# A fused two-layer mixer on one core: gate columns Z projected in the attention pairs, the state stage reordered, and the X tiles' weight sums made by GpSimd

## The chip, the cores and the metric

One core of a Trainium2 chip runs the whole program as one launch. The metric is device time in microseconds (us), lower is better. TensorE (PE) does the matrix products, VectorE (DVE) and ScalarE (ACT) the elementwise work, GpSimd (POOL) and SyncE (SP) issue DMAs. Everything is float32.

## The reference, cut to what matters

Three blocks follow one another over 256 tokens of width 2048. The change lies in the first, which mixes neighbourhood attention with a state-space part:

```python
p = h @ w_in                                   # h: 256 x 2048; columns Q, gate A, Z, K, V, X|B|C, dt
pc = hc @ w_in[:, base:]                       # the same for the 256 context tokens (K, V, X, B, C, dt alone)
ya = neighbourhood_attention(q, k, v, kc, vc, rpb) * silu(gate_a)
xs, B, C = silu(dw_conv(X|B|C));  dt = softplus(dt_raw + dt_bias)
y_ssd = bidirectional_ssd(...)                 # 8 groups, each 256 columns of X and Z, 128 of B, 128 of C
yz = (y_ssd + d * xs) * silu(z)                # z = Z columns of p
yb = yz * rsqrt(mean(yz * yz, per group) + EPS) * ssm_norm_g
out = concatenate([ya, yb]) @ w_out
```

So Z is used only at the end of each group of the state part, and depends on nothing in it.

## The kernel before

The engines run programs of their own, written out by hand in order, and meet at semaphores. Weight tiles of 2048 x 256 (2 MB) go through four slots `w[0..3]` in SBUF. The SP queue loads a slot as soon as PE has counted enough finished products in `acc_full`; the counts of each stage stand in `PHASES` (how many products a round has, and after which of them each slot is free).

The attention stage is eight pairs of heads (`na(i)`). Each pair has four weight tiles (Q, gate, K, V) and six units (`na_unit`), because K and V are also projected for the context tokens. A unit is one 256 x 256 x 2048 product in seven instead of eight block products of 128 x 128 x 1024 (56 matmuls with 128 moving columns), for which VectorE makes three block sums of the weights (`sums_one`, `sums_two`, placed in `w[3]`, counted in `na_t`) and combines the seven results afterwards (`na_combine`). ScalarE copies the results out of PSUM (`na_staging`). Between the units PE does the scores, transposes and values of the pair before. GpSimd loads the second layer's modulation weights through `xT` in the background, VectorE adds them up (`late_part`).

The state stage is eight groups (`ssd(g)`). From group 1 on, PE's order in a group is: X in four parts (`ssd_x`, seven block products with 256 moving columns, sums made by VectorE's `x_weights`), and between them the work of the group before: pairs of B and C (`s_cb`), state products (`s_st`), `ssd_within` 0 to 3 and `ssd_across`. Then B and C of this group (`featured`), Z in two halves of 16 matmuls with 256 moving columns (`tokened`), the transposes of the group before's result (`ssd_features`), and the transposes of this group's X and B into `wide` and `bank[5]` (counted in `s_xt`). VectorE's order is `x_weights`, `to_the_end`, `mask_cb`, `all_heads` (`decays` and `weights` for four heads, counted in `s_wm`), the X results, five-tap convolutions (`conv`, `conv_silu`), `combine` (the group before's result, which ends with `s_yz` and the scaling by `rz`), and at the end of the group the copies out of the transposes.

After group 7 PE starts the output projection (`out_first`, `out_half`) beside the last group's state work. The slot loads of that stage are in `out_proj` on SP.

Of the kernel before, what the change touches and what calls it, by code (L numbers as in the profile page):

```python
# [115 lines left out]
def build(nc, ins, out, scratch):  # L116
    x_scratch = nc.dram_tensor("x_columns", (P, DC * T), F32, kind="Internal").ap()
    y_scratch = nc.dram_tensor("na_columns", (P, DC * T), F32, kind="Internal").ap()
    f_scratch = nc.dram_tensor("ssd_columns", (P, DC * T), F32, kind="Internal").ap()
    with ExitStack() as ctx:  # L120
        program(nc, ctx, ins, out, scratch, x_scratch, y_scratch, f_scratch)


def program(nc, ctx, ins, out, scratch, x_scratch, y_scratch, f_scratch):
# [48 lines left out]

    IDENT, ANTI, ONES, BIG_GE = const("ident"), const("anti"), const("ones"), const("big_ge")
    FOLD = const("fold")
# [34 lines left out]
    staged0, partial0 = L(7, P), L(2, P)  # L210
    yout = L(2, T)
    late_rows = L(32)
# [86 lines left out]
    PHASES = [("na", 8, 12, [2, 4, 8, 12]), ("ssd", 8, 8, [4, 6, 8, 8]), ("out", 4, 4, [2, 2, 4, 4]),  # L299
# [77 lines left out]
    def na_filled(n, whole=True):  # L377

        return 12 * (n // 4) + (2, 4, 8, 12)[n % 4] - (0 if whole else 1)
# [28 lines left out]
    def loads(s, phase, i):  # L408
        g = GROUPS[phase]
        extra = 0  # L410
        if s == 1:
            extra = 16 * (i + 1) if phase == "ssd" else (16 * 8 if g > GROUPS["ssd"] else 0)
        if s == 3 and g > GROUPS["ssd"]:
            extra = -16 * 8
        extra += 16 * ((3, 3, 2, -8)[s] + EARLY[s])
        return 16 * (g + 1) + 16 * i + extra
# [8 lines left out]
    early_taken, late_taken, late_sum, late_added, x_moved, y_saved, y_back, wdt_in = (sem(n) for n in ("early_taken", "late_taken", "late_sum", "late_added", "x_moved", "y_saved", "y_back", "wdt_in"))  # L425
# [9 lines left out]
    def names(prefix, *which):  # L435
# [3 lines left out]
    (na_ss, na_rs, na_lnfree, na_kq, na_hk_in, na_sc, na_max, na_p, na_pn, na_pt, na_pts, na_po, na_y,  # L439
     na_g) = names("na", "ss", "rs", "lnfree", "kq", "hk_in", "sc", "max", "p", "pn", "pt", "pts", "po", "y", "g")  # L440
    (d_full, d_x, d_abs, d_log, d_a, d_cs, d_csout, d_rows, d_rowsb, d_store, d_toend, csb_in) = names(
        "dt", "full", "x", "abs", "log", "a", "cs", "csout", "rows", "rowsb", "store", "toend", "csb_in")
# [10 lines left out]
    (na_ge, s_ce, s_cl, s_zl, s_ze, sc_e, g2_x, g2_l, sb_ge, ch_ge) = (  # L453
        sem(f"sig_{n}") for n in ("na", "ssd_c", "ssd_cl", "ssd_zl", "ssd_z", "sc", "g2_x", "g2_l", "sb", "ch"))
# [12 lines left out]
    def _(gp):  # L467
# [25 lines left out]
        iterations(gp, 8, late_chunks)  # L493


    @block.sync
    def _(sp):
# [39 lines left out]
        def slot_free(phase, i, s):  # L537

            if isinstance(i, int) and i == 0:
                prev = EARLIER[phase]  # L540
                if phase == "ssd":
                    return sp.wait_ge(acc_full, na_filled((30, 31, 29)[s]))
# [24 lines left out]
        for n in (0, 2, 1, *range(3, 32)):  # L567
# [4 lines left out]
            at = (COL_Q, COL_GATE, COL_K, COL_V)[n % 4] + (n // 4) * TILE  # L572
# [8 lines left out]
            if n % 4 == 1 and n > 4:  # L581
                na_biases(n // 4 - 1)
        na_biases(7)

        def ssd(i):
            at = [columns(i, COL_X), columns(i, COL_Z)]
            half = [COL_B + i * P, COL_C + i * P] if isinstance(i, int) else [
                sp.snap(i * P + COL_B), sp.snap(i * P + COL_C)]
            slot_free("ssd", i, 0)
            load(0, w_in[:, :, ds(at[0], TILE)])  # L590
# [3 lines left out]
            slot_free("ssd", i, 2)  # L594
            load(2, w_in[:, :, ds(at[1], TILE)])
# [3 lines left out]
        def out_proj(i):  # L599

            at = [sp.snap(i * (2 * TILE) + n * TILE) if not isinstance(i, int) else (2 * i + n) * TILE for n in range(2)]
            for s in range(SLOTS):
# [4 lines left out]
                load(s, w_out[s % 2][:, :, ds(at[s // 2], TILE)])  # L607
                if is_first(i) and s == 0:

                    sp.wait_ge(y_saved, 16 * 8)  # L610
                    sp.dma_start(yT[:, 0:DC, :].rearrange("p a b -> p (a b)"), y_scratch).then_inc(y_back, 16)
                    sp.wait_ge(f_saved, 16 * 6)
# [55 lines left out]
    def _(pe):  # L668
# [145 lines left out]
        def na_values(a, h):  # L814
            pe.wait_ge(na_pts, 2 * a + h + 1)
            pe.wait_ge(n_made, 6 * a + 6)
# [22 lines left out]
        def na_unit(i, u, midway=None):  # L839
# [43 lines left out]
        def na(i):  # L883
# [22 lines left out]
            na_unit(i, 5, lambda: na_sums(i, 2, ksq[:, 1, :]))  # L906

# [34 lines left out]

        def ssd_x(g, part):
# [5 lines left out]
            if part == 0:  # L949
                pe.wait_ge(s_made, 12)  # L950
                product(a, quarter(0, 0, 1), XC(0, 0))
                last = product(b, quarter(0, 1, 1), XC(0, 1))
            elif part == 1:
                pe.wait_ge(x_t, 3 * g - 1)
                product(a, t2, XC_SUM[2])
                last = product(b, quarter(0, 0, 0), XC_SUM[3])
# [4 lines left out]
            else:  # L961
                pe.wait_ge(x_t, 3 * g)
# [3 lines left out]
        def ssd(g):  # L966
            first = is_first(g)
            s = g - 1
            loaded(0, "ssd", g)
            if first:  # L970
                dst = accumulate("ssd", 0, g)

                featured(dst[:, :], 0, 0, T + TC, None, range(EIGHT))
                na_scores(7, 0)
                featured(dst[:, :], 0, 0, T + TC, None, range(EIGHT, DC)).then_inc(acc_full, 3)
# [3 lines left out]
                featured(dst[:, :], 0, 1, T + TC, None, range(EIGHT))  # L979
                na_values(7, 0)  # L980
                na_transposes(7, 1)
                featured(dst[:, :], 0, 1, T + TC, None, range(EIGHT, DC)).then_inc(acc_full, 1)
# [3 lines left out]
            else:  # L986
                ssd_x(g, 0)
                pe.wait_ge(s_xtk, g)
                pe.wait_ge(s_silu, 4 * g)
                for jb in range(2):  # L990
                    last = mm(bank[2][:, jb * T:(jb + 1) * T], bT[:, jb * P:(jb + 1) * P], cmT[:, :])
                last.then_inc(s_cb, 1)
                ssd_x(g, 1)
# [28 lines left out]
            pe.wait_ge(s_silu, 4 * g + 3)  # L1022
            if not first:
                pe.wait_ge(s_t1, 2 * s + 2)
            for tb in range(4):
                for c in range(2):
                    tr(wide[:, tb * TILE + c * P:tb * TILE + (c + 1) * P], xc[:, c, tb * P:(tb + 1) * P])
            for jb in range(2):
                last = tr(bank[5][:, jb * P:(jb + 1) * P], bT[:, T + jb * P:T + (jb + 1) * P])
            last.then_inc(s_xt, 1)  # L1030

        def out_half(cb, ch, half):
# [4 lines left out]
            for kc in range(DC):  # L1037
# [4 lines left out]
        def out_first(cb, ch):  # L1042
# [3 lines left out]
            out_half(cb, ch, 0)  # L1046

        def ssd_apply(s, beside):
            ssd_across(s)
            for r in range(4):  # L1050
                if r == 2:
                    beside()
                ssd_within(s, r)
# [27 lines left out]
        iterations(pe, 8, ssd)  # L1081
        pe.wait_ge(s_xtk, 8)
        pe.wait_ge(s_silu, 32)
        for jb in range(2):
            last = mm(bank[2][:, jb * T:(jb + 1) * T], bT[:, jb * P:(jb + 1) * P], cmT[:, :])
        last.then_inc(s_cb, 1)
        pe.wait_ge(y_back, 16)
        out_first(0, 0)
# [5 lines left out]
        last.then_inc(s_st, 1)  # L1094
        out_first(0, 1)
        ssd_apply(7, lambda: out_first(1, 0))
        out_first(1, 1)
# [362 lines left out]
    def _(act):  # L1460
# [154 lines left out]
        for i in range(8):  # L1615
            na(i)
# [1309 lines left out]
```

## Time and profile before

| | |
|---|---|
| median of 3 runs | 2649.34 us (2647.27 to 2649.52) |
| profiled execution, its own time | 2646.37 us |
| span of that execution | 2644.7 us |
| granted TensorE clock, mean | 0.998 |
| PE / DVE / ACT / POOL busy | 98% / 65% / 18% / 2% |
| HBM | 171 GB/s over the span |

The profile comes from one execution. Its start times are us from the start of the span. A line in the timeline view is a run of like instructions on one engine: start, duration from the first one's start to the last one's end, line of the kernel, what is written from what, and count. A float32 matmul of the program is two MATMUL instructions in these views, so a count of 64 is 32 matmuls. Idle time before a run stands in brackets with what ended it.

### The profile page before, as it was taken

How to read it: one execution, taken by the hardware profiler on the slowest of the kernel's cores; microseconds unless marked ns; L12 is line 12 of the kernel's file. 1: busy time of each engine (PE TensorE's matmuls, PEld its weight loads, DVE VectorE, ACT ScalarE, POOL GpSimd, SP SyncE). 2: the span in 40 equal slices, each digit the busy share in tenths (PEclk: the TensorE clock that was granted, in tenths of full speed). 3: DMA queues.
4: the chain of work that ended last, by engine and by line, in shares of the span. 5: the costliest groups of instructions: out<-in, count | busy, mean ns of one | idle time of the engine just before them, and what ended most of it. 6: DMA issues, size and time to landing. Idle time of an engine off the chain costs nothing. (4 is left out here: it accounts for less than half of the span.)

```text
span 2644.7 us, 41302 instructions
## 1 busy us (share of the span) xinstructions
PE 2592.1 (98%) x17269; PEld 2305.3 (87%) x17269; DVE 1713.3 (65%) x2832; ACT 476.6 (18%) x922; POOL 60.9 (2%) x85
## 2 busy tenths in 40 slices
PE   5899999999999999999999999999999999999999
PEld 2399999999996877777778998888889999999999
DVE  6878778878775666666655535555566655556643
ACT  2121111212121222222220002111111112122211
POOL 1000000000000000000000000000000000000000
PEclk9999999999999999999999999999999999999999
DMA  9956666557554333333354546655654555555542
GB/s 379 366 168 224 197 218 202 189 187 242 193 170 141 97 104 111 115 115 115 115 207 159 171 149 191 188 152 170 190 165 155 154 165 149 152 156 156 166 149 74
DMA packets 382238, 453.96 MB, mean 172 GB/s; under 512 B 20884, under 2 KB 352264, under 8 KB 381064
## 3 DMA queue, kind: packets, MB, share of 16 engines
q1 hardware_dynamic: 350176, 352.03, 43.5%
q0 software_dynamic: 21776, 83.89, 8.8%
q10 hardware_dynamic: 10136, 15.86, 1.7%
q8 instruction: 117, 1.92, 0.3%
q14 instruction: 33, 0.27, 0.0%
HBM read 443.56 MB, written 8.19 MB: 171 GB/s over the span
## 5 line engine op out<-in xcount | busy, mean ns | idle before, releaser
L670 PE MATMUL bank<-hT,w 128*128 128x128 f32 (+2 forms) x4192 | 653.7, 314 | 4.2 <-ACT hT L1462 2.7
L670 PEld LDWEIGHTS bank<-hT,w 128*128 128x128 f32 x4192 | 548.4, 192 | 101.4 <-issue 87.4
L670 PE MATMUL bank<-yT,w 128*128 128x128 f32 (+1 forms) x3776 | 526.4, 299 | 1.5 <-DVE yT L2459 1.0
L670 PEld LDWEIGHTS bank<-yT,w 128*128 128x128 f32 x3776 | 493.2, 192 | 23.5 <-DVE yT L2459 1.2
L670 PE MATMUL bank<-w,hT 128*128 128x256 f32 (+2 forms) x2816 | 485.9, 332 | 3.3 <-ACT hT L1462 2.2
L670 PEld LDWEIGHTS bank<-w,hT 128*128 128x128 f32 x2816 | 438.8, 191 | 49.0 <-issue 9.5
L1462 ACT ACTIVATE work<-bank 128x512 f32<-128x512 f32 (+3 forms) x294 | 150.8, 521 | 1191.1 <-PE bank L670 1093.1
L1462 ACT ACTIVATE work<-work 128x512 f32<-128x512 f32 (+4 forms) x287 | 166.0, 584 | 279.4 <-DVE work L2309 156.1
L2134 DVE SCALAR_TENSOR_TENSOR work<-xT,silc,work 128x512 f32<-128x512 f32 x240 | 180.3, 751 | 28.2 <-DMA xT<-in_ada_w 21.4
L670 PE MATMUL bank<-work,hT 128*128 128x256 f32 x768 | 168.5, 379 | 0.0
L670 PEld LDWEIGHTS bank<-work,hT 128*128 128x128 f32 x768 | 145.4, 190 | 19.5
L2570 DVE TENSOR_TENSOR work<-w 128x2048 f32<-128x2048 f32 x16 | 36.7, 2292 | 152.8 <-PE bank L670 139.6
L670 PE MATMUL bank<-hT,work 128*128 128x128 f32 x1136 | 134.9, 275 | 0.0
L670 PEld LDWEIGHTS bank<-hT,work 128*128 128x128 f32 x1136 | 130.8, 192 | 0.0
L2524 DVE TENSOR_TENSOR work<-yT 128x128 f32<-128x128 f32 x37 | 10.8, 293 | 178.5 <-ACT yT L1462 178.5
L670 PEld LDWEIGHTS bank<-w,yT 128*128 128x128 f32 x1024 | 116.9, 192 | 3.8 <-issue 3.8
L670 PE MATMUL bank<-w,yT 128*128 128x128 f32 x1024 | 118.2, 275 | 0.0
L670 PE MATMUL bank<-work 128*128 128x256 f32 (+2 forms) x368 | 103.2, 408 | 2.9 <-DVE work L2495 1.6
L2309 DVE SCALAR_TENSOR_TENSOR work<-work,colp 128x512 f32<-128x512 f32 (+1 forms) x128 | 87.7, 685 | 15.0
L1462 ACT ACTIVATE yT<-bank 128x512 f32<-128x512 f32 (+1 forms) x63 | 35.6, 566 | 253.4 <-PE bank L670 221.9
L670 PEld LDWEIGHTS bank<-work 128*128 128x128 f32 x368 | 64.0, 191 | 17.6 <-issue 9.1
L670 PE MATMUL wide<-w,work 128*2 128x512 f32 x128 | 58.4, 604 | 14.3 <-DMA w<-in_ada_w 14.3
(253 smaller groups left out, 2541.8 us busy)
## 6 DMA issues: line engine op xcount, KB each, us to landing
w<-in_na_ssd_w_in SPq DMA_DIRECT2D x47, 2048.0 KB, 11.3
xT<-in_ada_w POOLq DMA_DIRECT2D x64, 1024.0 KB, 8.8
w<-in_sc_w_in SPq DMA_DIRECT2D x32, 2048.0 KB, 13.5
w<-in_w_in SPq DMA_DIRECT2D x32, 2048.0 KB, 10.7
w<-in_na_ssd_w_out SPq DMA_DIRECT2D x16, 2048.0 KB, 9.5
w<-in_na_ssd_w_in SPq DMA_DIRECT2D x18, 1024.0 KB, 8.9
w<-in_sc_w_out SPq DMA_DIRECT2D x8, 2048.0 KB, 8.6
w<-in_w_out SPq DMA_DIRECT2D x8, 2048.0 KB, 8.8
```

Source lines behind the costliest of these rows:

```text
L670: return nc.tensor.matmul(dst, lhsT, rhs, start=start, stop=stop, skip_group_check=free)
L1462: return nc.scalar.activation(*args, **kw)
L2134: last = v.scalar_tensor_tensor(out=aacc[:, block, :], in0=aring[:, at, kc, :], scalar=silc[:, k:k + 1], in1=aacc[:, block, :], op0=ALU.mu ...
L2309: last = v.scalar_tensor_tensor(out=o, in0=tap(k), scalar=col(f"conv_w{k}", c), in1=o, op0=ALU.mult, op1=ALU.add)
L2524: v.tensor_tensor(u[:, 0, :], p(0), p(2), ALU.add)
L2570: link(v.tensor_tensor(sums_wide[:, 0, :, :], q(0, 1), q(0, 0), ALU.subtract))
```

## The change

1. Each attention pair gets a fifth tile and a seventh unit for Z (`na_unit(i, 6)`). Its result, in the buffer `qraw`, goes to a scratch tensor in HBM (`gate_store`) and comes back in the state stage (`gate_rows`). The tile rotation is over five tiles instead of four, so every tile's place in the slots moves.
2. The Z products and their slot load leave the state stage. ScalarE takes the exponential from the SBUF copy.
3. PE's transposes of X and B (`ssd_turned`) move from the end of group g into part 0 of group g+1, the pair products (`ssd_pairs`) from before part 1 into its middle. VectorE's copies out of them move to the start of the next group, and the scaling by `rz` goes behind `conv(g, 2)`. The rows of cumulative sums (`cs_rows`) are fetched earlier.
4. `x_weights` moves from VectorE to GpSimd, with the same four subtractions.
5. Around the output projection's start, the column half order is changed, and its slot 2 is loaded already in group 1.

```diff
-    PHASES = [("na", 8, 12, [2, 4, 8, 12]), ("ssd", 8, 8, [4, 6, 8, 8]), ("out", 4, 4, [2, 2, 4, 4]),
+    PHASES = [("na", 8, 14, [2, 4, 8, 12]), ("ssd", 8, 6, [4, 6, 4, 4]), ("out", 4, 4, [2, 2, 4, 4]),
@@ gpsimd
+        def x_weights(g):
+            t1, t2, t4 = (x_places[:, m, :, :] for m in range(3))
+            gp.wait_ge(w_loaded[0], loads(0, "ssd", g))
+            nc.gpsimd.tensor_tensor(t1, quarter(0, 0, 0), quarter(0, 0, 1), ALU.subtract).then_inc(x_t, 1)
+            gp.wait_ge(x_t, 4 * g - 3)
+            nc.gpsimd.tensor_tensor(t2, quarter(0, 1, 0), t1, ALU.subtract).then_inc(x_t, 1)
+            nc.gpsimd.tensor_tensor(quarter(0, 0, 0), quarter(0, 1, 0), quarter(0, 0, 0), ALU.subtract).then_inc(x_t, 1)
+            gp.wait_ge(x_t, 4 * g - 2)
+            nc.gpsimd.tensor_tensor(t4, quarter(0, 1, 1), t2, ALU.subtract).then_inc(x_t, 1)
+        gp.wait_ge(late_taken, 64)
+        for g in range(1, 8):
+            x_weights(g)
@@ sync: the pairs' tiles, and the state stage's loads
-        for n in (0, 2, 1, *range(3, 32)):
+        for n in (0, 2, 1, *range(3, 40)):
-            at = (COL_Q, COL_GATE, COL_K, COL_V)[n % 4] + (n // 4) * TILE
+            at = (COL_Q, COL_GATE, COL_K, COL_V, COL_Z)[n % 5] + (n // 5) * TILE
...
-            if n % 4 == 1 and n > 4:
-                na_biases(n // 4 - 1)
+            if n % 5 == 1 and n > 5:
+                na_biases(n // 5 - 1)
...
-            slot_free("ssd", i, 2)
-            load(2, w_in[:, :, ds(at[1], TILE)])
@@ tensor
-            j = (0, 1, 2, 2, 3, 3)[u]
-            n, k = 4 * i + j, 12 * i + 2 * u
-            s, turned = na_slot(n), j == 3
+            j = (0, 1, 2, 2, 3, 3, 4)[u]
+            n, k = 5 * i + j, 14 * i + 2 * u
+            s, turned = na_slot(n), j > 2
...
+            na_unit(i, 6)
...
             if part == 0:
                 product(a, quarter(0, 0, 1), XC(0, 0))
+                ssd_turned(g - 1)
                 last = product(b, quarter(0, 1, 1), XC(0, 1))
             elif part == 1:
-                pe.wait_ge(x_t, 3 * g - 1)
+                pe.wait_ge(x_t, 4 * g - 1)
                 product(a, t2, XC_SUM[2])
+                ssd_pairs(g - 1)
...
-            loaded(2, "ssd", g)
-            for tb in range(2):
-                dst = accumulate("ssd", 6 + tb, g)
-                tokened(dst[:, 0:TILE], 2, tb).then_inc(acc_full, 1)
@@ scalar
+        def gate_store(a):
+            act.wait_ge(n_made, 7 * a + 7)
+            act.dma_start(z_scratch[:, 2 * a * T:(2 * a + 2) * T], qraw...).then_inc(z_saved, 16)
+        def gate_rows(g):
+            act.dma_start(zraw..., z_scratch[:, ds(at, 2 * T)]).then_inc(z_back, 16)
...
             if first:
                 rows_of_dt()
+                gate_rows(g)
+                cs_rows(g)
             conv_exp(g, 3)
...
-            cs_rows(g)
@@ vector
+            na_combine(i, 6, qraw)
...
-                x_weights(g, link)
+                turned(s)
                 to_the_end(s)
...
             conv(g, 2, link)
             if first:
                 ends_of_dt()
+            else:
+                scaled(s)
             conv_silu(g, 2, link)
@@ tensor, after group 7
+        out_first(1, 0)
+        ssd_turned(7)
+        ssd_pairs(7)
+        out_first(1, 1, range(EIGHT))
...
+        ssd_within(7, 2)
+        ssd_across(7)
+        ssd_within(7, 3)
+        loaded(1, "out", 0)
+        pe.wait_ge(f_back, 32)
+        out_half(0, 0, 1, range(14))
         ssd_features(7)
```

On PE, from the end of group 0 to the state products in group 1, the program before has this order (one row is a run of matmuls; L673 are transposes, `w,hT` with 256 columns is Z, `yT,xT` and `yT,w` are part 1 of X):

```order
L670 MATMUL bank<-w,hT 128x256 x32
L673 MATMUL wide<-cst,work 128x128 x8
L673 MATMUL bank<-cst,work 128x128 x2
L670 MATMUL bank<-hT,w 128x256 x16
L670 MATMUL bank<-work 128x256 x2
L670 MATMUL bank<-yT,xT 128x256 x8
L670 MATMUL bank<-yT,w 128x256 x8
L670 MATMUL bank<-w,work 128x256 x4
```

and the changed program this one:

```order
L694 MATMUL bank<-hT,w 128x256 x8
L697 MATMUL wide<-cst,work 128x128 x8
L697 MATMUL bank<-cst,work 128x128 x2
L694 MATMUL bank<-hT,w 128x256 x8
L694 MATMUL bank<-yT,xT 128x256 x8
L694 MATMUL bank<-work 128x256 x2
L694 MATMUL bank<-yT,w 128x256 x8
L694 MATMUL bank<-w,work 128x256 x4
```

The 32 Z matmuls are gone, the ten transposes stand after the first eight matmuls of part 0, and the two pair matmuls after the first eight of part 1.

On VectorE, from the end of `combine` in group 1 to the end of the group, before (L2451 is the scaling by `rz`, L2459 the features out of the transposes, L2494 and L2495 the copies of the transposed X and B; L2307 and L2309 are a convolution, L2115 a silu):

```order
L2448 TENSOR_TENSOR work<-work 128x512
L2451 TENSOR_SCALAR work<-work 128x256 x2
L2115 TENSOR_TENSOR work<-work 128x512
L2307 TENSOR_SCALAR work<-work,colp 128x512
L2309 SCALAR_TENSOR_TENSOR work<-work,colp 128x512 x4
L2115 TENSOR_TENSOR work<-work 128x512
L2307 TENSOR_SCALAR work<-work,colp 128x256
L2309 SCALAR_TENSOR_TENSOR work<-work,colp 128x256 x4
L2115 TENSOR_TENSOR work<-work 128x256
L2459 TENSOR_SCALAR work<-bank,colp 128x256 x2
L2494 COPY work<-wide 128x1024
L2495 COPY work<-bank 128x256
```

and after the change:

```order
L2483 TENSOR_TENSOR work<-work 128x512
L2158 TENSOR_TENSOR work<-work 128x512
L2354 TENSOR_SCALAR work<-work,colp 128x512
L2356 SCALAR_TENSOR_TENSOR work<-work,colp 128x512 x4
L2488 TENSOR_SCALAR work<-work 128x256 x2
L2158 TENSOR_TENSOR work<-work 128x512
L2354 TENSOR_SCALAR work<-work,colp 128x256
L2356 SCALAR_TENSOR_TENSOR work<-work,colp 128x256 x4
L2158 TENSOR_TENSOR work<-work 128x256
L2496 TENSOR_SCALAR work<-bank,colp 128x256 x2
L2535 COPY work<-wide 128x1024
L2536 COPY work<-bank 128x256
```

The scaling (now L2488) stands behind the third convolution instead of ahead of it. The copies L2535 and L2536 now belong to the next group, whose PE transposes they wait for.

## Rows read from the trace of the kernel before

**Rows 1.** The page, busy time of each engine.

```profile
PE 2592.1 (98%) x17269; PEld 2305.3 (87%) x17269; DVE 1713.3 (65%) x2832; ACT 476.6 (18%) x922; POOL 60.9 (2%) x85
```

**Rows 2.** Waits of PE after 150 us: us in total, times, longest.

```profile
PE bank L670 <- DVE work L2495: 1.6, 1, 1.6
...
PE bank L670 <- ACT work L1462: 1.3, 1, 1.3
...
PE bank L670 <- DVE yT L2459: 1.0, 1, 1.0
```

**Rows 3.** Timeline of PE: Z in group 7, and unit 0 of pair 7.

```profile
1352.20 13.98 PE L670 MATMUL bank<-w,hT 128*128 128x256 f32 x64
1366.02 0.60 PE L673 MATMUL bank<-cst,work 128*128 128x128 f32 x4
...
714.52 3.74 PE L670 MATMUL bank<-hT,w 128*128 128x128 f32 x32
...
727.03 1.88 PE L670 MATMUL bank<-work 128*128 128x512 f32 x4
```

**Rows 4.** Windows: one whole group; PE, PEld, DVE, ACT, POOL busy, clock, DMA.

```profile
1231.50:1299.50 68.00, 68.00 (x304) 53.66 (x303) 44.72 (x97) 15.90 (x32) 0.00 (x0) 1.00 0.37 112
```

**Rows 5.** Timeline of group 7, which starts at 1299.51.

```profile
1299.51 7.07 PE L670 MATMUL bank<-hT,w 128*128 128x256 f32 x32
...
1306.42 1.03 PE L670 MATMUL bank<-work 128*128 128x256 f32 x4
...
1309.02 1.93 DVE L2367 TENSOR_SCALAR w<-work 128x256 f32<-128x256 f32 x8 [0.78 <-DMA work<-cs_rows]
...
1312.74 0.42 DVE L2384 TENSOR_TENSOR w<-w 128x256 f32<-128x256 f32 x1
...
1315.91 1.00 PE L670 MATMUL bank<-work,w 128*128 128x64 f32 x8
...
1325.45 3.67 PE L670 MATMUL bank<-hT,xT 128*128 128x256 f32 x16
...
1340.70 0.69 DVE L2448 TENSOR_TENSOR work<-work 128x512 f32<-128x512 f32 x1
...
1345.58 0.60 ACT L1462 ACTIVATE work<-bank 128x512 f32<-128x512 f32 x1 [8.46 <-PE bank L670]
...
1347.47 0.62 DVE L2451 TENSOR_SCALAR work<-work 128x256 f32<-128x256 f32 x2 [6.08 <-ACT work L1462]
...
1349.29 3.44 DVE L2309 SCALAR_TENSOR_TENSOR work<-work,colp 128x512 f32<-128x512 f32 x4
```

**Rows 6.** DMAs of the X tile in group 6, issue to landing.

```profile
DMA to landing us min/median/max: 8.2/8.2/8.2
```

**Rows 7.** Two-operand work of VectorE (128x1024, 128x2048, beside GpSimd's DMAs), and those DMAs.

```profile
L2401 DVE TENSOR_TENSOR xT<-w,xT 128x1024 f32<-128x1024 f32 x7 | 8.6, 1225 | 0.2
...
861.06 2.29 DVE L2167 TENSOR_TENSOR yT<-hT 128x2048 f32<-128x2048 f32 x1
...
L2134 DVE SCALAR_TENSOR_TENSOR work<-xT,silc,work x240: 744/752/755, 159.5 to 815.0; 128x512 f32<-128x512 f32 x120
...
L478 POOL DMA_DIRECT2D xT<-in_ada_w x64: 748/748/757, 121.3 to 801.6; - x64
```

**Rows 8.** Timeline at the end of group 0 and start of group 1.

```profile
876.38 13.98 PE L670 MATMUL bank<-w,hT 128*128 128x256 f32 x64
...
882.35 1.31 ACT L1462 ACTIVATE work<-work 128x256 f32<-128x256 f32 x3 [5.35 <-DMA cs_rows<-work]
...
891.75 0.85 ACTq L1661 DMA_DIRECT2D work<-cs_rows  x2
...
900.67 1.92 DVE L2367 TENSOR_SCALAR w<-work 128x256 f32<-128x256 f32 x8 [0.66 <-DMA work<-cs_rows]
```

**Rows 9.** Attention bias DMAs of one pair on SP, and their landing.

```profile
686.45 8.25 SPq L564 DMA_DIRECT2D work<-in_na_rpb  x4
...
DMA to landing us min/median/max: 11.9/12.1/12.6
```

More of the change, by code:

```diff
@@ L611, in out_proj @@
                     sp.dma_start(yT[:, 0:DC, :].rearrange("p a b -> p (a b)"), y_scratch).then_inc(y_back, 16)
+                if not (is_first(i) and s == 2):
+                    load(s, w_out[s % 2][:, :, ds(at[s // 2], TILE)])
+                if is_first(i) and s == 0:
                     sp.wait_ge(f_saved, 16 * 6)
@@ L941, in rows_of_dt, with ssd_turned, ssd_pairs @@
             last.then_inc(d_rows, 1)
+        def ssd_turned(s):
+            pe.wait_ge(s_silu, 4 * s + 3)
+            wait(pe, s_t1, 2 * s)
+            for tb in range(4):
+                for c in range(2):
+                    tr(wide[:, tb * TILE + c * P:tb * TILE + (c + 1) * P], xc[:, c, tb * P:(tb + 1) * P])
+            for jb in range(2):
+                last = tr(bank[5][:, jb * P:(jb + 1) * P], bT[:, T + jb * P:T + (jb + 1) * P])
+            last.then_inc(s_xt, 1)
+        def ssd_pairs(s):
+            pe.wait_ge(s_silu, 4 * s + 4)
+            for jb in range(2):
+                last = mm(bank[2][:, jb * T:(jb + 1) * T], bT[:, jb * P:(jb + 1) * P], cmT[:, :])
+            last.then_inc(s_cb, 1)
         def ssd_x(g, part):
@@ L987, in ssd @@
                 ssd_x(g, 0)
+                ssd_x(g, 1)
                 pe.wait_ge(s_xtk, g)
[L989 to L993, printed above, removed]
                 pe.wait_ge(s_xe, g)
@@ L1014, in ssd, with out_half @@
                 rows_of_dt()
-            loaded(2, "ssd", g)
-            for tb in range(2):
-                dst = accumulate("ssd", 6 + tb, g)
-                tokened(dst[:, 0:TILE], 2, tb).then_inc(acc_full, 1)
             if not first:
                 ssd_features(s)
[L1022 to L1032, printed above, removed]
+        def out_half(cb, ch, half, chunks=range(DC)):
             dst = bank[cb][:, ch * T:(ch + 1) * T]
-            for kc in range(DC):
+            for kc in chunks:
                 last = mm(dst, w[2 * cb + half][:, kc, ch * P:(ch + 1) * P], yT[:, half * DC + kc, :],
@@ L1045, in out_first @@
                 pe.wait_ge(acc_free, BANKS["out"] + cb - 1)
[L1046 to L1053, printed above, removed]
+            out_half(cb, ch, 0, chunks)
         def ssd_across(s):
@@ L1081, in _ @@
         iterations(pe, 8, ssd)
-        pe.wait_ge(s_xtk, 8)
[L1083 to L1088, printed above, removed]
+        pe.wait_ge(y_back, 16)
+        out_first(1, 0)
+        ssd_turned(7)
+        ssd_pairs(7)
+        out_first(1, 1, range(EIGHT))
+        pe.wait_ge(s_xtk, 8)
         pe.wait_ge(s_xe, 8)
@@ L1094, in _ @@
         last.then_inc(s_st, 1)
+        out_first(1, 1, range(EIGHT, DC))
+        ssd_within(7, 0)
+        out_first(0, 0)
+        ssd_within(7, 1)
         out_first(0, 1)
-        ssd_apply(7, lambda: out_first(1, 0))
-        out_first(1, 1)
+        ssd_within(7, 2)
[4 more added lines that the diff above has]
+        out_half(0, 0, 1, range(14))
         ssd_features(7)
@@ L1106, in _ @@
             for ch in range(2):
-                last = out_half(cb, ch, 1)
+                last = out_half(cb, ch, 1, range(14, DC) if cb + ch == 0 else range(DC))
             last.then_inc(acc_full, 2)
@@ L1587, in na @@
             a = i - 1
+            if not first:
+                gate_store(a)
             na_staging(i, 0, 0)
@@ L1747, in ssd @@
             A(e, e, ACT.Exp, scale=-1.0).then_inc(s_ze, 1)
-            cs_rows(g)
-            if not first:
-                feature_store(g - 1)
         ssd_setup()
+        act.wait_ge(z_saved, 16 * 8)
         iterations(act, 8, ssd)
@@ L1984, in looped @@
             if n > 2:
-                with dve.Fori(2, n) as i:
+                with dve.Fori(2, n - last) as i:
                     chain = Chain(dve, dve_link, start + (i - 2) * steps, steps)
@@ L1988, in looped @@
                     chain.close()
-                total[0] = start + (n - 2) * steps
+                total[0] = start + (n - last - 2) * steps
+                for i in range(n - last, n):
+                    body(i, link)
         v.memset(prm, 0.0).then_inc(params_zeroed, 1)
@@ L2502, in _ @@
         combine(7, link)
+        scaled(7)
         features(7)
```

141 lines of the change are left out of this document (76 added, 65 removed).

## The prediction

> **What bounds the kernel now.** The page comes first: TensorE is busy 98% of the span, VectorE 65% [rows 1]. The view of PE's waits then says where it stands idle: the three waits that belong to the stages changed here are 1.6, 1.3 and 1.0 us, once each [rows 2]. All three lie in the handover from group 7 to the output projection. The windows say the same of one group: PE is busy 68.0 of 68.0 us, VectorE 44.7, ScalarE 15.9 [rows 4]. So the time is the sum of the matmuls, and the change can give only what it takes off that sum, and can lose wherever it makes PE wait. That is read from the timeline, as the slack of each partner.
>
> **Z in a seventh unit.** In the state stage Z starts at 1352.20 and the next work at 1366.02: 13.8 us for 64 instructions with 256 columns, 0.216 us each. A unit in the pairs starts at 714.52 and the next work at 727.03: 12.5 us for 112 instructions with 128 columns, 0.112 us each [rows 3]. Seven products instead of eight would give an eighth, but two narrow instructions cost a little more than a wide one, so 1.3 us is left. Eight times that is **−10.5 us**. This is the whole of the direct gain.
>
> The unit costs VectorE four weight sums of 1.2 us [rows 7] and a combination, some 7 us within 12.5 us that PE adds; hidden, since PE never waits for VectorE in the pairs. What moves besides is the bias fetch: its four DMAs take SP 8.3 us to issue and land 12 us later, some 19 us in all [rows 9]. They start one unit before the end of the pair now, so VectorE meets them about 18 us after their issue and waits some 1 to 2 us. PE needs that work more than 2 us later, so I cost it at nothing. If that cover is gone it is 1 to 2 us for each of seven pairs.
>
> **The X tile of group 0** is now loaded at the end of unit 5, with one unit (12.5 us) of cover and B and C right behind it in the queue. A 2 MB tile alone lands in 8.2 us [rows 6]; sharing could cost 0 to 3 us, once. I take 0.5.
>
> **Groups 1 to 7, the chain.** Let T be the time from a group's part 0. Before, a group is 68.0 us; after, 68.0 − 13.8 = 54.2. The transposes in part 0 (1.1 us) move everything behind them up to C back by 1.1. The partners, one by one, by the durations of [rows 5]:
> - Pairs to first weights. Before, the pair product is issued at T = 6.9, and VectorE's first `weights` ends at 1312.74 + 0.42, T = 13.65. Of that 0.8 was a wait for the DMA of `cs_rows`, ahead of the decays at 1309.02, that the earlier fetch takes away: 5.9 us from product to weights. After, the product comes at 6.9 + 1.1 + 3.45 = 11.5, so the weights are there at 17.4. PE wants them at 16.4 + 1.1 = 17.5. The margin of 2.7 us is down to nothing. I charge 0.07 us a group, **+0.5 us**; were the step 0.5 us longer it would be 3.5 us.
> - Combination and third convolution. The second half of the heads' work runs 2.0 us later than before, so `s_yz` comes at T = 43.9 instead of 41.9, and the silu behind it, of the same size as that row's 0.69 us, at 44.6. PE finishes B at 46.0 + 1.1 = 47.0, ScalarE copies until 47.7, the convolution takes 4.1 (to 51.9), the scaling 0.6 (to 52.5). PE's feature transposes, before at 66.5, are due at 66.5 − 13.8 + 1.1 = 53.8. Slack 1.3 us, and 3.2 us of idle time ahead of the convolution. Hidden. What the removed Z hid before is this very chain.
> - The third silu ends at T = 54.7, 0.5 into the next group; the transposes in part 0 ask for it at 3.5. The fourth is later by 4 us and asked for at 11.5. Hidden.
>
> **Group 0 to 1.** ScalarE still waits for the store of the cumulative sums and goes on at 882.35. Only then does it issue the gate rows and `cs_rows`. From its first `cs_rows` issue to VectorE's use of them takes 8.9 us (891.75 to 900.67) [rows 8], so they are there at about 882.8 + 8.9 = 891.7. Without Z, PE starts group 1 where Z starts now, at 876.4. VectorE is then ready for the rows at T = 8.7 + 1.1 + 3.45 = 13.3 (8.7 is where it stood in group 7 before it had to wait for them), that is at 889.7. It is 2.0 us late and has no margin: **+2.1 us**, once.
>
> **The handover after group 7.** The three waits of 3.9 us in all [rows 2] go. In their place: after the last `ssd_across` VectorE needs 5.7 us for `combine` and 2.1 for root and scaling, while PE has the last `ssd_within` and 28 matmuls, 0.85 + 28 × 2 × 0.216 = 6.9: about 1.0 us of wait ahead of the feature transposes. Their readers cost 1.0 again. Slot 3 can be loaded only behind them, where PE has 36 matmuls, 7.8 us, over a load of 8.2 us [rows 6] and its issue: 0.5 to 1.7. Sum 2.5 to 3.7. I take **0**; bounds −1 and +1.
>
> **The weight sums on GpSimd.** No row shows such an operation on GpSimd. The nearest are VectorE's own, 1.22 us for this size and 2.29 for twice the size [rows 7]; below the first I see no reason, and take 2.29 as the upper end. Either way there is room: the X tile's load is issued after part 3, at T = 25.9 + 1.1 + 3.7 = 30.7, and lands at 38.9. Part 1 of the next group asks for three of the sums at 54.2 + 8.0 = 62.2, so three may take 23 us, 7.8 each. The time of the sums is hidden whichever end holds, and the 4.9 us that VectorE gives up lie off PE's path. Cost **0**.
>
> **The sum.** −10.5 + 0.5 + 0.5 + 2.1 + 0 = −7.4. The profiled execution took 2646.4, which gives 2639.0; the median of the runs stands 3.0 above that execution, so I forecast **2642.0** (−0.28%).
>
> **Rivals.**
> - *VectorE and GpSimd get in each other's way.* Both would be reading two operands from SBUF from T = 38.9, just where VectorE has 10.4 us of work left before the scaling (5.0 of `combine`, 0.7 of silu, 4.1 of convolution, 0.6 of scaling) and 14.9 us to do it in: 4.5 spare. If one waits for the other, VectorE loses four times the price p of a sum, less some 1.6 us beside instructions with one SBUF operand: PE would wait 4p − 6.1 in each of groups 1 to 6. At p = 1.22 that is nothing, at 2.29 it is 3.1, in all 18 us: **2660**. PE waits from p = 1.5 on, and from p = 2.1 on (2.1 us a group) the kernel is slower by over 0.2%. For it: GpSimd and VectorE never compute at once in this trace, so nothing excludes it. Against it: VectorE's two-operand additions beside GpSimd's DMA instructions (0.75 us each) keep to 744 to 755 ns [rows 7], though those do not read tiles. A rule of the Trainium skill speaks for it: "SBUF — State Buffer" (Who interferes with whom) says that a VectorE instruction with two SBUF inputs and a GpSimd instruction that reads SBUF exclude each other for the whole instruction. By "GPSIMD Engine Reference" (Performance versus the Vector engine) a subtraction of twice this size takes GpSimd 4497 ns; an estimate of 2.25 us for this one would put the kernel at 2659. No run here shows either.
> - *The thin margins give way.* Weights 0.5 us later than reckoned in seven groups, biases 1 us late in seven pairs, 2 us more at the handover: +7 to +10, so nothing is left: **2649**.
> - *GpSimd is far slower than both rows*: above 7.8 us a sum, PE waits 3 us a group for each further one: 2670 and more. Only the distance to the rows speaks against it.
> - *No new wait at all*, and the old 3.9 us gone: **2636**.
>
> **Chances.** Forecast 0.45 (2638 to 2646), shared access 0.34 (2650 to 2664), margins gone 0.12, GpSimd far slower 0.04, no wait 0.05. A measurement of this kernel tells about 0.2%, 5.3 us, from no change. The forecast lies only 2 us past that, so 0.07 of its 0.45 counts as the same, as does 0.03 of the shared access (p near 2) and 0.10 of the margins. Faster 0.43, same 0.20, slower 0.37. The range takes in both large cases, **2637 to 2663**, and leaves out the far slower GpSimd, the best case and the tails.
>
> **What would show it.** Right: an attention pair longer by 12.5 us and still without PE waits; groups of 54.2 us; PE waiting once for `cs_rows` in group 1; about 4 us of waits at the handover; GpSimd's four sums between T = 39 and 50, with VectorE's convolution still at 0.75 us an instruction. Wrong: the feature transposes of groups 1 to 6 waiting for the scaling, with VectorE's gaps or durations grown beside GpSimd's sums (shared access); `ssd_within` 0 waiting for the weights (margin); part 1 waiting for the sums (slow GpSimd); PE waits in the pairs (biases, or the slots' new rotation).

## The result and the profile after

The changed kernel is slower: 2674.6 us median of 5 runs (2662.6 to 2675.0), the ratio to the kernel before (2649.1 us in the same set) is 1.0082, 95% interval 1.007 to 1.0093. The medians alone would give 1.0096, because the runs lie in two clumps, two at 2663 to 2664 us (granted clock 0.993) and three at 2675 (0.989), and the median falls in the upper one; the profiled execution, 2664.35 us, is one of the first. Both clumps are told of below.

The page, busy time of each engine (answers to [rows 1]):

```profile
PE 2596.9 (98%) x17653; PEld 2314.8 (87%) x17653; DVE 1778.2 (67%) x2884; ACT 480.8 (18%) x914; POOL 134.7 (5%) x113
```

VectorE is busy 65 us longer, though it gave away 34 us of sums (7 times 4.9); the eight Z units in the pairs add about 56 us at the prediction's 7 us each, which leaves an estimated 43 us that are no new work. The view of PE's waits after 150 us begins with a line for the scaling, where [rows 2] had nothing of the kind. Of the handover's 3.9 us in [rows 2] there are left 0.86, in that line's sum, and the 1.0 for yT; the wait for the modulation column was 1.1 us in the kernel before too:

```profile
PE bank L697 <- DVE work L2488: 13.6, 7, 2.8
...
PE bank L694 <- DVE mod L2203: 1.1, 1, 1.1
PE bank L694 <- DVE yT L2496: 1.0, 1, 1.0
...
PE bank L694 <- DVE w L2430: 0.8, 2, 0.6
```

L2488 is the scaling by `rz`, and L697 stands for the feature transposes, which cannot start without it. Six of the seven waits are in groups 1 to 6. Windows of these groups, from one X load to the next (columns as in [rows 4]; the forecast was 54.2 us each):

```profile
1010.83:1066.50 55.67, 54.71 (x239) 41.33 (x238) 45.99 (x91) 15.23 (x29) 10.31 (x4) 1.00 0.36 104
1066.50:1127.12 60.62, 57.65 (x239) 43.51 (x238) 47.84 (x93) 15.46 (x29) 10.55 (x4) 0.94 0.32 96
1127.12:1186.19 59.07, 56.56 (x239) 42.48 (x238) 47.29 (x93) 15.46 (x29) 10.54 (x4) 0.97 0.33 98
1186.19:1243.57 57.38, 54.94 (x239) 41.35 (x238) 47.15 (x93) 15.34 (x29) 10.98 (x4) 1.00 0.35 101
...
sum 348.72, PE 335.07 PEld 252.59 DVE 282.41 ACT 92.28 POOL 64.31; mean PE 55.85 PEld 42.10 DVE 47.07 ACT 15.38 POOL 10.72
```

The timeline shows why the scaling is late. `combine` of one group on VectorE, GpSimd's four sums, and PE behind them:

```profile
1311.44 0.69 DVE L2477 TENSOR_TENSOR work<-work,bank 128x512 f32<-128x512 f32 x1
1312.27 1.89 DVE L2479 TENSOR_TENSOR work<-work 128x512 f32<-128x512 f32 x1
1314.20 2.72 DVE L2480 TENSOR_TENSOR work<-work 128x512 f32<-128x512 f32 x1
1316.95 2.72 DVE L2158 TENSOR_TENSOR work<-work 128x512 f32<-128x512 f32 x1
1319.71 2.73 DVE L2483 TENSOR_TENSOR work<-work 128x512 f32<-128x512 f32 x1
1322.36 0.68 DVE L2158 TENSOR_TENSOR work<-work 128x512 f32<-128x512 f32 x1
...
1310.74 2.87 POOL L502 TENSOR_TENSOR xT<-w 128x1024 f32<-128x1024 f32 x1 [47.64 <-DMA w<-in_na_ssd_w_in]
1313.69 2.68 POOL L504 TENSOR_TENSOR xT<-w,xT 128x1024 f32<-128x1024 f32 x1
1316.34 2.79 POOL L505 TENSOR_TENSOR w<-w 128x1024 f32<-128x1024 f32 x1
1319.09 2.80 POOL L507 TENSOR_TENSOR xT<-w,xT 128x1024 f32<-128x1024 f32 x1
...
1327.66 0.66 PE L697 MATMUL bank<-cst,work 128*128 128x128 f32 x4 [2.24 <-DVE work L2488]
```

The two engines take turns. GpSimd's sums end at 1313.61, 1316.37, 1319.13 and 1321.89 us, and each of the four VectorE operations beside them ends 0.55 us after one of these. An operation of 0.69 us ([rows 5]) shows 2.72, because it stands through a sum. The operation ahead, which has one operand in PSUM, keeps 0.69. Four operations last 10.06 us instead of 2.76; of these 7.3 us 2.24 come out as PE's wait, so some 5 were spare. In group 1 part of the turns falls where VectorE had to wait for ScalarE anyway, and PE waits 0.81.

Where a clock fell, the timeline of PE shows it in the instructions behind the wait:

```profile
1152.56 0.72 PE L697 MATMUL bank<-cst,work 128*128 128x128 f32 x4 [2.38 <-DVE work L2488]
1153.24 5.27 PE L694 MATMUL bank<-hT,w 128*128 128x256 f32 x16
...
1211.49 0.66 PE L697 MATMUL bank<-cst,work 128*128 128x128 f32 x4 [2.24 <-DVE work L2488]
1212.21 3.69 PE L694 MATMUL bank<-hT,w 128*128 128x256 f32 x16
```

The same 16 matmuls take 5.27 us behind the one wait and 3.69 behind the other: the clock falls behind some of these waits. So the six groups lose 12.7 us in waits, and PE is busy 8.5 us longer in them (335.1 us against 326.5 in the best version below, e10). Of these 8.5 us 7.4 are in the three groups whose granted clock is below 1.00; the others, at clock 1.00, are 0.3 to 0.5 us longer each.

### The profile page after: what moved, and what is told of

Its sections match the earlier page's. It is cut to its first block and busy times, and to the rows that moved or that the text cites. A ratio compares the mean times of both kernels' runs of the same rounds, so it can differ in the third digit from the quotient of the medians.

```text
span 2662.7 us, 42135 instructions
## 1 busy us (share of the span) xinstructions
PE 2596.9 (98%) x17653; PEld 2314.8 (87%) x17653; DVE 1778.2 (67%) x2884; ACT 480.8 (18%) x914; POOL 134.7 (5%) x113
## 5 line engine op out<-in xcount | busy, mean ns | idle before, releaser
L694 PE MATMUL bank<-hT,w 128*128 128x128 f32 (+2 forms) x4192 | 663.4, 316 | 4.3 <-ACT hT L1489 2.7
L694 PE MATMUL bank<-w,hT 128*128 128x128 f32 (+2 forms) x2688 | 419.9, 316 | 3.3 <-ACT hT L1489 2.2
L694 PEld LDWEIGHTS bank<-w,hT 128*128 128x128 f32 x2688 | 386.3, 192 | 36.4 <-issue 9.5
L694 PEld LDWEIGHTS bank<-w,yT 128*128 128x128 f32 x1536 | 174.7, 192 | 3.8 <-issue 3.8
L694 PE MATMUL bank<-w,yT 128*128 128x128 f32 x1536 | 176.7, 275 | 0.0
L480 POOL DMA_DIRECT2D xT<-in_ada_w x64 | 47.9, 749 | 763.0 <-DVE work L2177 709.3
L2250 DVE TENSOR_TENSOR work<-work 128x128 f32<-128x128 f32 x55 | 16.0, 292 | 98.8 <-ACT work L1489 98.7
```

Of the source, the lines that this page charges most:

```text
L480: gp.dma_start(aring[:, c % 2, :, :], src).then_inc(late_in[c % 2], 16)
L694: return nc.tensor.matmul(dst, lhsT, rhs, start=start, stop=stop, skip_group_check=free)
L2250: v.tensor_tensor(partial0[:, 0, :], p(0), p(3), ALU.add)
```

## The experiments

My theory: **shared access**, VectorE's operations on SBUF and GpSimd's sums exclude each other while `combine` runs. Rivals: the chain is too long without Z whoever makes the sums; and, for the 12 us between the clumps, falls in the groups against a fall elsewhere. The runs of the kernel before beside these kernels had medians of 2648.6 to 2649.2 us.

**e1_sums_after_scaling: the sums back on VectorE, elsewhere.**

```diff
-        for g in range(1, 8):
-            x_weights(g)            # GpSimd
...
             else:
                 scaled(s)
+            if not first and not (isinstance(g, int) and g == 7):
+                x_weights(g + 1)    # VectorE; group 1's sums stand ahead of steps_of_dt
```

> The changed kernel with one thing moved: the four weight sums of the next group's X tile are made by VectorE again, behind the two scalings of the gated rows (in group 0 ahead of the time steps), GpSimd makes none. Shared access (my theory): VectorE's 128x512 operations of combine take 0.69 us again instead of up to 2.73, the scaling comes about 5 us earlier than PE wants it, the waits of TensorE for the scaling (2.83, 2.38, 2.24 us and so on in groups 1 to 6, 12.7 us together) are gone, and the four sums take 4 times 1.23 us in time that VectorE has. At least 2663 - 12.7 = 2650 us; if the falls of the granted clock are a consequence of these waits, groups of 54.3 to 55.5 us, clock 0.998, and 2638 to 2645 us. Rival (chain too long once the Z unit is gone, whoever makes the sums): the scaling is as late as before, 2.2 us of wait in each group, 2660 us or more.

Measured: 2647.2 us median of 12 runs, ratio 1.0001 (0.9987 to 1.0016). No wait for the scaling in groups 1 to 6, groups of 54.4 to 55.0 us at clock 1.00: shared access holds, the long chain falls. But the median is above the 2638 to 2645 us that I named for this case: the runs spread from 2640.5 (clock 0.998) to 2660.0 (0.992), five of them at 2654.6 or more. Of the other seven two are at 2640.5, four at 2645 and one at 2649; no profile shows what parts these. The profiled one, 2657.2 us, is of the five and shows where the clock fell in it, in windows of 10 us at the end of the attention (columns as above) and in PE's timeline:

```profile
930.00:940.00 10.00, 10.00 (x36) 5.84 (x36) 4.17 (x6) 0.00 (x0) 0.00 (x0) 1.00 0.03 3
940.00:950.00 10.00, 8.94 (x54) 8.83 (x53) 5.87 (x12) 1.09 (x2) 0.00 (x0) 0.70 0.92 293
950.00:960.00 10.00, 10.00 (x49) 10.00 (x49) 4.30 (x4) 0.26 (x1) 0.00 (x0) 0.50 0.47 160
...
941.54 25.35 PE L679 MATMUL bank<-w,hT 128*128 128x64 f32 x128 [1.06 <-DVE mod L2188]
966.68 16.23 PE L679 MATMUL bank<-hT,w 128*128 128x512 f32 x32
```

In the profiled execution of the changed kernel the same instructions, behind the same wait, kept the clock:

```profile
941.18 14.47 PE L694 MATMUL bank<-w,hT 128*128 128x64 f32 x128 [1.07 <-DVE mod L2203]
```

These are `steps_of_dt`. The granted clock of 0.50 is the lower level, 1.2 GHz. It costs 10.9 us in them and 2.3 in the unit behind them (16.23 us against 13.95), 13.2 us together, about the distance of the clumps.

**e2_gpsimd_later: GpSimd starts behind the scaling.**

```diff
             gp.wait_ge(w_loaded[0], loads(0, "ssd", g))
+            if g > 1:
+                gp.wait_ge(s_yn, 2 * g - 2)
```

> The changed kernel with one wait more: GpSimd starts the sums of groups 2 to 7 only when VectorE has scaled the previous group's rows. Shared access: combine runs at 0.69 us per operation and TensorE doesn't wait for the scaling; the stretch moves to VectorE's product with the silu of unit 2 and to convolution 3, whose results are wanted 5 to 10 us later; they are late by up to 7 us, so that a wait of 0 to 3 us in each group comes up there. 2640 to 2660 us, below the changed kernel's 2663. If GpSimd's sums only need to be anywhere but in combine, 2640 to 2645. Rival (chain too long): unchanged waits for the scaling, 2660 or more. Rival (GpSimd too slow in itself): the waits of TensorE name the sums' results (part 1 of the X product), over 2 us per group.

Measured: 2668.0 us, ratio 1.0074 (1.006 to 1.0089). That is outside the 2640 to 2660 us that I named, and above the changed kernel's lower clump. `combine` ran at 0.69 us an operation, the wait for the scaling went, and the turns came up in the third silu and the fourth convolution:

```profile
1329.70 1.56 DVE L2160 TENSOR_TENSOR work<-work 128x512 f32<-128x512 f32 x1 [1.49 <-ACT work L1491]
1331.18 2.44 DVE L2356 TENSOR_SCALAR work<-work,colp 128x256 f32<-128x256 f32 x1
1333.77 6.09 DVE L2358 SCALAR_TENSOR_TENSOR work<-work,colp 128x256 f32<-128x256 f32 x4
...
1350.65 1.80 PE L696 MATMUL bank<-work,w 128*128 128x64 f32 x8 [2.61 <-DVE w L2432]
```

PE now waits for the weights of `ssd_within`, 15.4 us in six groups:

```profile
PE bank L696 <- DVE w L2432: 15.4, 6, 2.6
```

The stall moves with the sums. The operation with a single tile operand (TENSOR_SCALAR) is stretched as well, from 0.41 us to 2.44, which the prediction's "two operands" did not say.

**e3_before_gpsimd_sums: the kernel before, with the GpSimd sums alone.** Its diff is the part of the change on `x_weights`.

> The kernel before with the GpSimd sums alone: the Z units stay in the state stage, scaling stays where it was. Shared access: the same operations of combine are stretched, to about 2.7 us each, 7 us together, and TensorE doesn't notice, since the Z unit of 14 us stands between the chain and the transposes of the scaled rows: no wait, the same time as before within 0.2% (2644 to 2652). Rival (shared access costs by itself, by a lower clock or by slower TensorE): slower by 0.2% or more.

Measured: 2648.7 us, ratio 1.0001 (0.9992 to 1.001). The operations are stretched just so, from 0.69 ([rows 5]) to:

```profile
1275.14 2.72 DVE L2450 TENSOR_TENSOR work<-work 128x512 f32<-128x512 f32 x1
```

and PE has no wait at all from 900 to 1340 us, since the Z unit stands behind the chain. So GpSimd's sums cost nothing as long as the Z unit covers the chain. The loss needs both: the sums on GpSimd and the chain without its cover.

**e4_sums_old_place: the changed kernel, `x_weights(g)` on VectorE at the start of the group, as before.**

> The changed kernel with the sums by VectorE at the place where the kernel before had them, the start of the group, ahead of the copies of the turned rows. The first three are wanted by part 1 of the X product 8.6 us into the group, when VectorE has only just ended the features of the group before (9.5 us): with 3.6 us for three of them TensorE waits about 4 us in each of groups 2 to 7, and the weights behind them (margin 0.15 us below zero) come 4.9 us later, of which the first wait has paid 4. About 6 to 7 groups times 5 us on top of 2638: 2668 to 2680 us, with waits for the sums, not for the scaling. Clock: if waits of this size make it fall, 0.985 to 0.99. Rival (VectorE's place does not matter): under 2650.

Measured: 2669.3 us, ratio 1.0065 (1.0049 to 1.0081). PE waits for the sums, not the scaling:

```profile
PE bank L679 <- DVE w L2434: 12.9, 7, 5.1
```

That is 5.1 us in group 1 and 0.7 to 1.4 in the others, where I had said 4; PE never waited for the weights behind them. Three of four runs, at 2669 to 2670, are longer by the length of the fall in `steps_of_dt`, and the profiled one shows it; the fourth is at 2658.2. So my range of 2668 to 2680 was met by luck: the waits were smaller than I reckoned, and the fall, which I had not counted, made up for them. With the Z units gone the sums could not stay at this place; e1 shows that they could stay on VectorE.

**e5_wait_behind_steps: e1, and PE's wait for the last modulation column moved.**

```diff
         def steps_of_dt():
             pe.wait_ge(wdt_in, 16)
-            pe.wait_ge(mod_ready, 9)
...
         def sums_of_dt():
+            pe.wait_ge(mod_ready, 9)
             pe.wait_ge(d_a, 1)
```

> The kernel with the sums behind the scaling, and TensorE's wait for the last modulation column taken from ahead of the time-step products to behind them (the wait of 1.06 us in front of the 128 products with 64 columns, in which the clock stood at half for about 29 us in the profiled execution of that kernel). If the wait brings the fall of the clock there: no execution of 2655 us or more any more, clock 0.995 to 0.998, 2638 to 2645 us, 0.2% to 0.4% below before. If the fall comes with the products with few columns, wherever the wait is: still about half of the executions at 2653 to 2659 us, and the median 2645 or more.

Measured: 2641.8 us (2639.0 to 2645.7, 10 runs), ratio 0.9977 (0.9967 to 0.9986). The upper clump is gone, and the version is faster than the kernel before. In its profile the scaling is ready before PE wants it:

```profile
1193.26 0.61 DVE L2485 TENSOR_SCALAR work<-work 128x256 f32<-128x256 f32 x2
...
1195.05 0.60 PE L682 MATMUL bank<-cst,work 128*128 128x128 f32 x4
```

**e6_steps_among_units: e5, with the 128 small products in four pieces between parts of the next unit's.**

> The same, and the time-step products no longer stand in one piece of 14.5 us: each 32 of them are followed by 8 of the 32 products with 512 columns of unit B... in four pieces each. If the piece of small products is what lets the clock fall: no execution above 2646 us; 2637 to 2643 us, unless the time steps come so late to VectorE (about 10 us later) that group 0 waits for them, 1 to 5 us. If neither wait nor piece matters: executions of 2655 us and more stay.

Measured: 2657.5 us, ratio 1.0036 (1.0022 to 1.0049). I had named 2637 to 2643, or 1 to 5 us more. It tells nothing on the small products: the edit made PE wait 3.2 us ahead of the first piece, then 2.1 us for the late time steps and 1.4 us for a silu, and in windows of 10 us the clock stood at 0.82 behind the first of these and 0.83 behind the second.

**e7_gpsimd_copies: copies instead of subtractions on GpSimd** (`nc.gpsimd.tensor_copy` of the first operand); it leaves out the subtractions, so the X tiles get other weights.

> The changed kernel, with GpSimd's four subtractions replaced by copies of their first operand in the same form, 128x1024, at the same places (so the products of the X tiles get other weights: this part of the computation is left out). If a GpSimd instruction shuts VectorE out of SBUF only when it has two operands there: VectorE's operations beside it take 0.69 us, no wait of TensorE for the scaling, 2638 to 2660 us. If any GpSimd instruction over SBUF does: the same alternation with stretched operations of about 1 us plus the copy's own time, and TensorE waits for as much as the copies last longer than 1.6 us each; at a copy of 1.2 to 2.3 us this is 0 to 2 us in each of groups 2 to 7.

Measured: 2641.3 to 2657.0 us, median 2654.6, six of ten runs in the upper clump (the profiled one with clock 0.50 in `steps_of_dt`), the others at 2641 to 2646. No wait for the scaling in groups 1 to 6. The turns are still there, shorter:

```profile
1197.36 1.50 POOL L504 COPY xT<-w 128x1024 f32<-128x1024 f32 x1
...
1197.99 1.41 DVE L2480 TENSOR_TENSOR work<-work 128x512 f32<-128x512 f32 x1
```

A GpSimd copy with one operand shuts VectorE out too. At 0.7 us a turn the loss stays within the 5 us to spare; at 2.0 us it does not.

**e8_two_more_sums: the fourth sum made three times on GpSimd.**

> The changed kernel, with GpSimd making the fourth sum three times: six instructions in each group in place of four. Shared access with strict turns: two more operations of VectorE are stretched from 0.69 to about 2.73 us, the scaling comes 4.1 us later, and TensorE's waits for it grow from 2.2 to 6.3 us in each of groups 1 to 6: 2663 + 6 times 4.1 = 2688 us at the same clock, up to 2710 with falls of the clock behind each wait. If the wait had another cause (the length of the chain itself): within 0.2% of the changed kernel.

Measured: 2702.0 us, ratio 1.0209 (1.0193 to 1.0225). The waits, in the view of PE's waits:

```profile
PE bank L700 <- DVE work L2491: 38.5, 7, 6.8
```

37.6 us of it are in groups 1 to 6, 6.3 each in the mean (4.9 in the first), as foretold. The profiled execution, 2697.0 us, is 32.7 above that of the changed kernel, and 24.9 of these are waits for the scaling; its clock is lower too (0.987 against 0.993).

**e9_after_wait_behind_steps: the changed kernel with e5's one line moved.**

> The changed kernel with one line moved: TensorE's wait for the last modulation column stands behind the time-step products. The sums stay on GpSimd. If the executions of 2675 us are the ones in which the clock falls in the time steps, and the wait in front of them lets it fall: no execution above 2668 us, all at 2659 to 2666 with clock 0.992 to 0.994, and TensorE's waits for the scaling as before, 12 to 14 us. Rival (the 2675 come from somewhere else, the falls of the groups): both clusters stay, median near 2674.

Measured: 2662.1 us (2660.1 to 2665.7, 8 runs), ratio 1.0045 (1.003 to 1.006). The waits for the scaling are as before:

```profile
PE bank L697 <- DVE work L2488: 12.8, 6, 2.9
```

So the upper clump of the changed kernel goes with this wait. No run of that clump was profiled; that it is the fall in `steps_of_dt` follows from its length and from the profiles of e1, e4 and e7.

**e10_sums_split: e5, with the first two sums ahead of convolution 2 and the other two behind the scaling.**

```diff
             conv_silu(g, 1, link)
+            x_weights(g + 1)           # t1, t2
             conv(g, 2, link)
             ...
                 scaled(s)
-            x_weights(g + 1)
+            x_weights_rest(g + 1)      # the other two
```

> The version with the sums on VectorE and the wait moved, and the four sums in two pairs: two ahead of convolution 2, where VectorE stands idle for 3.7 us in each group, two behind the scaling as now. The product with the silu of unit 2 comes 2.4 us earlier, and TensorE's wait of 0.16 us ahead of the turned rows goes. Groups of 54.7 us in place of 55.0: 1 to 2 us less than that version, 2638 to 2642 us, 0.25% to 0.4% below before. Should it be slower, the two sums ahead of convolution 2 (2.5 us) made the scaling late again.

Measured: 2638.5 us (2636.4 to 2639.5, 6 runs), ratio 0.9952 (0.9933 to 0.997): the best version. PE has no wait in groups 1 to 6:

```profile
1173.22:1227.83 54.61, 54.48 (x239) 41.41 (x238) 44.44 (x97) 15.26 (x29) 0.00 (x0) 1.00 0.35 106
...
sum 327.19, PE 326.54 PEld 248.45 DVE 266.53 ACT 91.73 POOL 0.00; mean PE 54.42 PEld 41.41 DVE 44.42 ACT 15.29 POOL 0.00
```

**e11_scaling_old_place: e5, with `scaled(s)` back behind `combine`.**

> The version with the sums on VectorE and the wait moved, with the two scalings back in their old place, ahead of the silu product of unit 1 and convolution 2. VectorE then stands until ScalarE has the root of the mean square, about 5 us, and convolution 2, the sums and the silu product of unit 2 come after it: that product, wanted 4 us after the transposes of the scaled rows, is 2.3 us late where it was 0.16. If the new place of the scaling is worth what I think, 2 to 3 us of wait in each of groups 1 to 6, 12 to 18 us in all and falls of the clock on top: 2653 to 2668 us. Rival (the place is worth nothing): within 0.1% of that version, 2642.

Measured: 2653.6 us (2649.8 to 2655.6, 10 runs), ratio 1.0013 (1.0001 to 1.0025). That is 11.8 us above e5 by the medians, 9.5 by the ratios, since the two stood in different sets of runs. PE waits for the third silu, 10.7 us in six groups (1.9 each, 1.4 in the first). The new place of the scaling is worth about that. In the profiled execution (2650.3 us, clock 0.998) none of these groups had a fall of the clock; most of the others are 3 to 5 us longer at 0.995 to 0.997.

**e12_before_wait_behind_steps: the kernel before with e5's line moved.**

> The kernel before with only that line moved. No execution of the kernel before showed the fall in the time steps, so only the wait itself goes, 1.06 us, if something behind it doesn't take it up: 2647 to 2649 us, 0 to 0.05% below before, which tells how much of the gain of the best version is the change's own. If the wait matters to the clock elsewhere: 0.1% or more below.

Measured: 2647.3 us, ratio 0.9988 (0.9975 to 1.0), so within the noise it is the 1.06 us of wait and little else. In this set the kernel before itself showed the fall's length three times in 25 runs (2659.3 to 2660.7).

## Why the prediction was wrong

**The direct gain was right.** The store of each pair's attention rows in the kernel before, and in the changed one, by first and last start:

```profile
L1583 ACTq DMA_DIRECT2D na_columns<-work x8: 326/326/359, 256.6 to 837.8; - x8
```

```profile
L1610 ACTq DMA_DIRECT2D na_columns<-work x8: 326/326/345, 271.7 to 940.5; - x8
```

(668.8 − 581.2) / 7 = 12.5 us more per pair, without a wait of PE. A group without the sums on GpSimd is 54.6 us (e10) where I said 54.2: 2.4 us over six groups. It is the margin at the first weights, which I had charged with 0.07 us a group. From the matmuls ahead of the first `ssd_within` to that product it took 1.72 us before (it starts at 1315.91 in [rows 5]), and takes 2.03 in the changed kernel, 0.1 more being lost behind it:

```profile
1314.19 1.89 PE L670 MATMUL bank<-w,work 128*128 128x256 f32 x8
```

```profile
1170.66 1.89 PE L694 MATMUL bank<-w,work 128*128 128x256 f32 x8
1172.69 1.10 PE L694 MATMUL bank<-work,w 128*128 128x64 f32 x8
```

The biases and the X tile of group 0 cost nothing.

**The step that failed** is "The weight sums on GpSimd", cost 0. The duration was judged well (2.34 us undisturbed, against the 2.29 taken), and so was the chain: with the sums away from `combine` the scaling is about 1.2 us early (e5: it ends at 1193.87 us, the transposes start at 1195.05), where I had reckoned 1.3. What failed is that a busy GpSimd was taken as no burden to VectorE. This was the rival "VectorE and GpSimd get in each other's way", with 3.1 us a group; measured 2.1, and where I had said 4.5 us were spare it was 5. (Its remark that p = 2.1 gives 2.1 us a group does not follow from 4p − 6.1, which gives 2.3.) I gave it 0.34, for want of a row with both engines computing. The rule of the Trainium skill named there ("SBUF — State Buffer", Who interferes with whom) agrees with the timelines: an operation of 0.69 us lasts 2.72 beside a sum, and 0.69 where one of its operands is in PSUM. It asks only that GpSimd's instruction reads SBUF, so it covers e7's copy with one operand too. The VectorE operation with one tile operand that took turns in e2 (0.41 to 2.44 us) is beyond the rule as the prediction quoted it. The 4497 ns stands in the Trainium skill ("GPSIMD Engine Reference", Performance versus the Vector engine) for an addition; half of it is the prediction's estimate of 2.25 us, and the subtraction here took 2.34.

**What no case held** is the clock. Even the rival gave 2660, and the range ended at 2663. Of the 2674.6 − 2640.5 = 34 us between the changed kernel and the fastest runs of e1 (the same kernel without GpSimd's sums), 12.7 are waits for the scaling, about 8.5 are longer busy time in the groups behind such waits (7.4 of it where the clock fell), and 12 to 13 the fall in `steps_of_dt` of the upper clump. The first two come of the sums; the third does not, since e1 and e4, without GpSimd's sums, have it too. That the change with the sums on VectorE and the wait moved (e5, 2641.8 us) meets the forecast of 2642.0 is partly luck: terms that were off by about +2 us (the groups), −2 (the handover) and −1 (group 0 to 1) cancel in it.

**Why that fall is there** is settled in part. With PE's wait in its place it came in 3 of 5 runs of the changed kernel, 5 of 12 of e1, 3 of 4 of e4, 6 of 10 of e7 and none of 4 of e2, counted by time and seen as clock 0.50 in three profiles; in the kernel before in 3 of 73. With the wait moved it came in none of 46 (e5, e9, e10, e11, e12; left out are e8, whose spread hides it, and e6, which had a longer wait of its own there). So in these kernels the fall came only with the wait there. Why the same wait of 1.06 us seldom does it in the kernel before is open. PE runs the same list of matmuls in the last 37 us ahead of the wait in both. What differs is the Z units in the pairs further ahead, and the load beside the wait (295 GB/s in the changed kernel's 10 us from 940, 242 in those from 837 before), and no run took either away alone.

**The smaller terms.** Group 0 to 1: 0.6 us of wait where I said 2.1. Handover: 1.8 us of wait (0.86 and 0.97) against 3.9, so −2.1 where I said 0, outside my bounds of −1 and +1; slot 3 did not wait. (The sum there reads 28 × 2 × 0.216, which would be 12.1 us; its 6.9 belongs to 28 instructions, that is 14 matmuls, and 28 instructions in 6.26 us are what the changed kernel ran there.) The new place of the scaling, costed only through its margin, is worth about 10 to 12 us (e11).

## What to carry to other kernels

Work moved to GpSimd need not be off VectorE. Here each VectorE operation on SBUF beside a sum paid 2.0 us, nearly the sum's 2.34, so place such work where VectorE is idle or has slack of that size, or leave it on VectorE, which made these sums in 1.22 us. An edit that costs nothing under a covering unit (e3) can cost a stage without it: when a unit that covers a chain goes, cost every other edit on that chain again. And look for short waits of TensorE even where their sum is small, since the clock can make 13 us of 1 us.

## What the hardware showed that was not expected

- GpSimd's 128x1024 subtraction takes 2.34 us alone and 2.67 to 2.87 in turns with VectorE; its copy 1.04 alone and 1.50 in most turns. VectorE's 0.69 us operation takes 2.72 and 1.41 in these turns. An operation with one operand in PSUM kept 0.69 us beside them.
- The granted clock can fall behind a wait of TensorE as short as 1.06 us (e1: clock 0.50 for about 27 us by the windows, `steps_of_dt` 25.35 us against 14.47). Behind 2.24 us it fell in one group of the changed kernel and not in two others (5.05 and 3.69 us for the same matmuls), and behind six waits of up to 1.9 us it did not in the profiled execution of e11.
